# Other places for the second scan's steps and the samples' updates between the units of a feed-forward network

## What is computed

```python
x = x + mix
x = x + swiglu(rmsnorm(x, norm_ffn[layer]), ffn_w_up[layer], ffn_w_down[layer])
```

```python
o_inter = einsum('bthk,bhkv->bthv', qc * exp(b), S)
scores  = einsum('bthk,bshk,btshk->bhts', qc, kc, decay)
o_intra = einsum('bhts,bshv->bthv', scores, vc)
S_new   = S * exp(b_last) + einsum('bshk,bshv->bhkv', k_dec, vc)
```

## Time and profile before

| | us |
|---|---|
| median of 3 runs | 2445.24 (2444.88 to 2445.74) |
| the profiled execution | 2445.97 |
| its span | 2444.2 |
| PE busy | 2420.0 |
| POOL busy | 1180.9 |
| DVE busy | 988.5 |
| ACT busy | 875.2 |

### The profile page before, as it was taken

How to read it: one execution, slowest core, us unless ns; L and a number is a source line. 1 busy time by engine, 2 the same in 40 slices (tenths; PEclk the granted TensorE clock), 3 DMA queues, 4 the chain that set the end, 5 groups by cost and what they waited for, 6 DMA issues and landing times.

```text
span 2444.2 us, 37585 instructions
## 1 busy us (share of the span) xinstructions
PE 2420.0 (99%) x15528; PEld 2187.7 (90%) x15528; DVE 988.5 (40%) x1712; ACT 875.2 (36%) x1154; POOL 1180.9 (48%) x933
## 2 busy tenths in 40 slices
PE   9999999999999999999999999999999999999998
PEld 6899987787888988999999989988888889999998
DVE  4513246344445344433343434344443434323324
ACT  5431235343223355433333243254432324222223
POOL 3722147655555444635445550064455555554454
PEclk9999999999999999999999999999999999999999
DMA  9863363322324587322223274432232344222222
GB/s 326 308 224 138 143 249 124 127 70 78 117 78 136 175 277 265 124 78 87 87 70 104 92 275 167 160 97 78 78 126 94 113 151 142 87 95 96 88 86 87
DMA packets 102249, 335.91 MB, mean 137 GB/s; under 512 B 12288, under 2 KB 16192, under 8 KB 102080
## 3 DMA queue, kind: packets, MB, share of 16 engines
q1 hardware_dynamic: 102080, 333.52, 39.9%
HBM read 255.20 MB, written 76.16 MB: 136 GB/s over the span
## 4 chain that ended last, share of the span: by engine, by line
PE 90%; DVE 3%; POOL 3%; issue 1%; ACT 1%; POOLq 1%; DMA 1%; DVEq 0%; SPq 0%; ACTq 0%
PE ps L830 64%; PE ps L896 19%; POOL wl L1466 2%; POOLq L1472 1%; PE ps L936 1%; PE ps L992 1%; PE ps L990 1%; PE ps L912 0%; PE ps L1053 0%; PE ps L1050 0%; PE ps L996 0%; PE ps L947 0%; POOL rsA L1478 0%; POOL sq L1573 0%; DMA wr<-in_wblk 0%
## 5 line engine op out<-in xcount | busy, mean ns | idle before, releaser
L1466 POOL TENSOR_TENSOR wl<-wr,wh 128x512 fp32r<-128x512 f32 x656 | 869.1, 1353 | 592.1 <-ACT wh L1196 588.6
L830 PE MATMUL ps<-xh,wh 128*128 128x260 f32 (+2 forms) x3296 | 881.1, 322 | 5.2 <-DVE xA L1860 2.2
L830 PE MATMUL ps<-xl,wh 128*128 128x260 f32 (+2 forms) x3296 | 867.7, 318 | 0.0
L830 PE MATMUL ps<-xh,wl 128*128 128x260 f32 (+1 forms) x3280 | 866.1, 319 | 0.0
L830 PEld LDWEIGHTS ps<-xh,wh 128*128 128x128 f32 (+1 forms) x3296 | 543.1, 187 | 59.5 <-issue 17.0
L830 PEld LDWEIGHTS ps<-xl,wh 128*128 128x128 f32 (+1 forms) x3296 | 542.5, 187 | 44.7 <-issue 2.4
L830 PEld LDWEIGHTS ps<-xh,wl 128*128 128x128 f32 x3280 | 540.9, 188 | 44.4
L1196 ACT ACTIVATE wh<-wr 128x1024 fp32r<-128x1024 f32 (+1 forms) x332 | 343.4, 1046 | 380.5 <-DMA wr<-in_wblk 376.3
L896 PE MATMUL ps<-hidh,wh 128*128 128x260 f32 (+1 forms) x1024 | 275.2, 322 | 3.7 <-DVE hf L1873 1.4
L896 PE MATMUL ps<-hidl,wh 128*128 128x260 f32 (+1 forms) x1024 | 274.2, 321 | 0.0
L896 PE MATMUL ps<-hidh,wl 128*128 128x260 f32 (+1 forms) x1024 | 272.9, 320 | 0.0
(11 more groups left out here) (375 smaller groups left out, 2288.9 us busy)
## 6 DMA issues: line engine op xcount, KB each, us to landing
wr<-in_wblk SPq DMA_DIRECT2D x328, 512.0 KB, 3.7
split<-wh SPq DMA_DIRECT2D x64, 512.0 KB, 5.4
split<-wl SPq DMA_DIRECT2D x64, 512.0 KB, 6.4
wh<-split SPq DMA_DIRECT2D x64, 512.0 KB, 3.2
wl<-split SPq DMA_DIRECT2D x64, 512.0 KB, 4.2
xr<-in_xT SPq DMA_DIRECT2D x8, 260.0 KB, 6.4
xB<-in_xT SPq DMA_DIRECT2D x8, 260.0 KB, 5.4
out_yT<-xB SPq DMA_DIRECT2D x8, 260.0 KB, 2.2
```

Of the source, the lines that this page charges most:

```text
L830: mm = pe.matmul(ps[0:cols, b + c, 0:n], wt[:, w], xt[:, e:e + n], start=first, stop=end)
L1466: last = pool.tensor_tensor(lo[:, e], raw[:, e], hi[:, e].bitcast(F32), ALU.subtract)
```

## The change

Two tuples of places. The scan's three steps per chunk now come behind up units 0, 1 and 3 of its group instead of behind units 0 and 2 and behind down 3. The samples' pairs (4, 5) and (6, 7) now come behind up units 1 and 3 of group 8 instead of behind unit 2 and down 3. The groups, the steps themselves, all units and their banks stay.

```diff
-                       scan("s0", B, ((0, 0), (0, 2), (0, 4), (3, 4, 5, 6, 7))),
+                       scan("s0", B, ((0, 0), (0, 1), (0, 3), (3, 4, 5, 6, 7))),
                        {(7, 0): [("dma", "smp0")], (7, 1): [("q0",)]},
-                       {p: [("qs", 2 * i), ("qs", 2 * i + 1)] for i, p in enumerate(((7, 3), (8, 0), (8, 2), (8, 4)))},
+                       {p: [("qs", 2 * i), ("qs", 2 * i + 1)] for i, p in enumerate(((7, 3), (8, 0), (8, 1), (8, 3)))},
```

## The result

| | before | after |
|---|---|---|
| median of 13 runs each, us | 2445.55 (2443.61 to 2449.01) | 2451.79 (2449.40 to 2454.69) |
| ratio after to before | | 1.0023, 95% interval 1.0014 to 1.0031 |
| profiled execution, us | 2445.97 | 2449.40 |
| its span, us | 2444.2 | 2447.3 |

The changed kernel is slower by 0.23%, 5.6 us by the ratio. The forecast was plus 2.8, the range ended at 2450.0. The profiled execution is the fastest of after's 13 runs, 3.4 us above that of before.

A forecast was written before the change was run, and what follows sets the result against it. PE, 99% busy, was taken as the bound, so only its idle time could change. Terms 0.2 + 0.1 + 2.5 gave plus 2.8 us: 2448.8 against the profiled execution, given as 2448.0, range 2445.2 to 2450.0.

The forecast's parts named there:

- What bounds the kernel, and how little there is to win: Whole span: PE is 99% busy, about 3.5 us idle beside the moved steps; 0.2% faster (4.9 us) is out of reach.
- Step 2 moves, the wait moves with it: Scan in groups 3 to 6: up-unit waits for `xA` become down waits, minus 3.2 plus 3.2, restarts plus 0.2 us.
- `hidl` behind it, and GpSimd's hold on the port: Groups 3 to 5: VectorE's `hidl`, now behind step 2, waits only for GpSimd's instruction under way; plus 0.1 us in all.
- rival C: Groups 3 to 5: GpSimd keeps `hidl` out until `S`, `GS` and `wl` finish; 8.4 us more, 2456.4 us; chance 6%.
- Step 1 moves; the gate's product is on time by 1 us: Scan, third to second unit: PE's inputs and the third unit's silu product arrive in time; no cost.
- The samples' updates, plus 2.5: Group 8, after the second unit: PE waits for VectorE's state updates, late through GpSimd's queue; plus 2.5 us, bounds 2.2 to 3.3.
- Pair (6,7) covered: Group 8, fourth unit: updates and down 0's eviction end by 6.0 us, PE needs the bank at 7.8; no wait.
- Sum and chances: Whole kernel: plus 2.8 us; chances 88% within 0.2%, 10% slower, 2% faster.

The follow-up runs named there:

- e1: Before with only the scan's three steps moved, samples left in place: ratio to before 0.9998, mean span -0.1 us.
- e11: The changed kernel timed once more, on another chip, beside before: ratio to before 1.0024, mean span +5.6 us.
- e2: Before with only the samples' pairs (4,5) and (6,7) moved, scan left in place: ratio to before 1.0020, mean span +4.7 us.
- e6: Before with only the samples' pair (4,5) moved, to behind group 8's second unit: ratio to before 1.0016, mean span +4.5 us.
- e9: The changed kernel with GpSimd's scaling of states 2 and 3 one more weight block later: ratio to before 1.0031, mean span +8.1 us.
- e3: The changed kernel with ten unneeded 512-column matmuls in front of sample 4's wait: ratio to before 1.0014, mean span +2.6 us.

## Why the prediction was right or wrong

**What bounds the kernel, and how little there is to win:** right for this edit. Everything that moved was PE's idle time, and what follows it. But "PE stands still" was taken for the only way in which a move can cost time, and the clock was the second.

**Step 2 moves, the wait moves with it:** right in mechanism and size (plus 0.3 foreseen with `hidl`, 0.1 measured in e1, good to 0.9). The three waits it left are of 0.5, 0.9 and 0.6 us. Groups 3 to 7 took 210.27 us before (470.90 to 681.17) and 210.20 after (469.46 to 679.66). VectorE's chain and first eviction, then the down that waited for it, in the chain that ended last:

```profile
549.78 0.61 DVE xA L1860
550.43 5.81 PE ps L896 x24
```

**`hidl` behind it, and GpSimd's hold on the port:** right. Timelines of VectorE and GpSimd, group 4:

```profile
550.88 1.50 DVE L1879 TENSOR_TENSOR hidl<-hf,hidh 128x512 fp32r<-128x512 f32 x1
...
550.79 1.04 POOL L1550 TENSOR_TENSOR GS<-S,fx 128x512 f32<-128x512 f32 x1
551.79 2.99 POOL L1466 TENSOR_TENSOR wl<-wr,wh 128x512 fp32r<-128x512 f32 x2
```

`hidl` waits for the end of `GS` and gets in before the weight pair, whose first half it delays (2.99 us for two, instead of 2.5). It was done 1.95 us after down 4's start (550.88 + 1.50 = 552.38, against 550.43); the prediction had it between 1.2 and 2.4, and rival C needed more than 2.2. No later down waited.

**Step 1 moves; the gate's product is on time by 1 us:** right, nothing seen. ScalarE's extra table load and its silu:

```profile
577.93 1.28 ACT L1320 ACT_TABLE_LOAD   x1
579.22 0.63 ACT L1320 ACTIVATE sq<-sq 128x512 f32<-128x512 f32 x1
```

GpSimd's product of it was done at 582.26, and VectorE's `hf` at 582.83 had waited for PE's fourth unit and not for it: 0.6 us to spare, where 1 us was foreseen.

**The samples' updates, plus 2.5:** this is the step that failed, by what it left out. The wait, its place, its releaser and GpSimd's queue as its cause were right: 2.4 us of gap and 0.3 of slower steps in after's profile, and a rest of 2.4 (e11), 2.7 (e2) and 3.3 us (e6). The term was mis-sized because an idle PE was priced at its idle time alone. The rows of before showed stops of 0.9 and 1.1 us with the clock at 1.00 behind them, and the sum took that price for a stop of 2.4 us in front of the samples' narrow matmuls. Behind these comes a stretch at 0.50: 1.6 us more for the two units in after's profile, 1.7 or 3.4 us by the length of the stretch in the profiles, 1.2 (e6) to 3.3 us (e11) by the mean clocks. The bound for this term (3.3) had only 0.5 us for a restart and a bank in it. With 1.7 to 3.4 more, the sum would have been plus 4.5 to 6.2; measured were 5.6.

Would the trace of before have told? Not by its stops: one of 2.3 us, at 380.16 to 382.46, has wide matmuls behind it and the clock at 1.00 (table of stretches):

```profile
380.00:383.00 3.00, 0.86 (x4) 0.30 (x3) 0.00 (x0) 0.00 (x0) 2.25 (x2) 1.00 0.55 167
383.00:386.00 3.00, 3.00 (x14) 2.29 (x13) 0.00 (x0) 2.31 (x3) 0.00 (x0) 1.00 0.58 161
```

But the half-clock stretch at 1896 us behind layer 1's samples was in it, with its price of 1.7 us, and the prediction weighed no clock at all.

**Pair (6,7) covered:** right: PE has no wait there.

**Sum and chances.** Faster was rightly at 2%. "Slower by over 0.2%" got 10% through another mechanism (C), and the range ended 1.8 us too low. The rivals priced other waits; none priced a second cost of the wait that was forecast.

## What to carry to other kernels

When an edit gives a matmul-bound kernel a TensorE stop of some microseconds, above all one beside very narrow matmuls, price it as the stop plus a possible stretch at half clock behind it (here 1.7 or 3.4 us for a stop of 2.4): that other stops in the trace kept the clock is no promise for this one. Look through the whole trace of before for stretches at half clock and for what TensorE did ahead of them. A step moved nearer to its predecessor needs the queues of all its producers read out at the new place; here two 1 us instructions in the wrong order in GpSimd's queue were the whole loss. A stall that comes from a chain of fixed length is not removed by moving step and chain together, but by putting more TensorE work between the step and the first unit that needs what stands behind the chain.

## What the runs showed of the hardware

- TensorE's granted clock fell to 0.50 behind a stop of 2.4 us and the samples' narrow matmuls in four profiles out of four (after, e2, e6, e11), and behind a stop of 4.9 us in e9. It stayed at 1.00 behind stops of 0.9, 1.1 and 2.3 us with wide matmuls after them. It stayed down for 3.4 us in one profile (after) and 6.8 us in another of the same kernel (e11), so one stop has no fixed price. How much of it the stop makes and how much the narrow matmuls is open; in e2 the clock was down before they were through.
- It also fell without any stop in the record: in e3 behind 2.5 us of the samples' matmuls, and in layer 1 behind 2.7 us of such work, there in 21 of 39 places of the 13 profiles, with 1.7 us lost at each. A busy TensorE in the trace is not enough to keep the clock, and the same program loses it in one execution and not in the next.
- In both places looked at, a VectorE instruction with two operands in SBUF ended about 0.6 us after the end of the GpSimd instruction under way, and so went ahead of what GpSimd had next where it had more: `hidl` took 1.69 us at 490.30 and 1.50 us at 550.88, between `GS` and the weight pair, against 0.68 us alone.
